# Sums of squares in a transformer kernel: six of eight tiles gathered on VectorE before TensorE sums them

## The reference

```python
def rms_norm_2(x, g):
    xf = xf * lax.rsqrt(jnp.mean(xf * xf, axis=-1, keepdims=True) + RMS_EPS)
    return (xf * g.astype(jnp.float32)).astype(x.dtype)

def pre(x_in, i):
    return rms_norm_2(x_in, norm_pre[l, i]) * (1.0 + mod[:, i, 1]) + mod[:, i, 0]

def post_add(x_in, y, i, res_w):
    return x_in + res_w * mod[:, i, 2] * rms_norm_2(y, norm_post[l, i])
```

## Time and profile before

| | |
|---|---|
| median of 3 runs | 3460.66 us (3459.83 to 3464.83) |
| profiled execution, first to last instruction | 3460.6 us (the profile gives no other time for it) |
| TensorE busy | 98% |
| VectorE, ScalarE, GpSimd busy | 47%, 35%, 13% |
| mean granted TensorE clock | 0.993 |

### The profile page before, as it was taken

The page is one execution under the profiler, slowest core; times in us unless marked ns, Lnnn a source line. Parts: engine busy times, 40 slices in busy tenths (PEclk is TensorE's granted clock), DMA queues, the critical chain, the costliest instruction groups (busy, mean ns, idle before and its releaser), DMA issues.

```text
span 3460.6 us, 38984 instructions
## 1 busy us (share of the span) xinstructions
PE 3388.4 (98%) x16286; PEld 2652.6 (77%) x16286; DVE 1630.0 (47%) x2132; ACT 1223.9 (35%) x1770; POOL 432.9 (13%) x338
## 2 busy tenths in 40 slices
PE   8999999999999999999999999999999999999998
PEld 6755477788888888887587888878888876878886
DVE  5555566443335635564334534475446533452233
ACT  3364465332223232224533322233323245332222
POOL 0100012121220100112011100110101210210001
PEclk9999999999999999999999999999999999999999
DMA  5412643234333334223032344333422322222221
GB/s 191 146 43 84 186 177 133 110 128 146 142 138 113 107 137 136 74 110 116 19 122 98 128 146 146 134 114 110 151 104 68 123 91 68 86 86 98 97 89 58
DMA packets 78353, 393.43 MB, mean 114 GB/s; under 512 B 8416, under 2 KB 17120, under 8 KB 45024
## 3 DMA queue, kind: packets, MB, share of 16 engines
q1 hardware_dynamic: 66048, 370.41, 30.9%
q10 hardware_dynamic: 12128, 20.52, 1.7%
HBM read 372.02 MB, written 18.87 MB: 113 GB/s over the span
## 4 chain that ended last, share of the span: by engine, by line
PE 93%; DVE 3%; ACT 2%; issue 1%; DMA 0%; POOL 0%; SPq 0%; DVEq 0%; ACTq 0%; POOLq 0%
PE pb L705 22%; PE pb L707 22%; PE pb L706 22%; PE pb L612 3%; PE pb L673 2%; PE pb L674 2%; PE pb L610 2%; PE pb L681 2%; PE pb L869 1%; PE pb L887 1%; PE pb L737 1%; PE pb L848 1%; DVE wl L2013 1%; PE pb L1200 1%; PE pb L1150 1%
## 5 line engine op out<-in xcount | busy, mean ns | idle before, releaser
L2013 DVE TENSOR_TENSOR wl<-w,wh 128x2048 fp32r<-128x2048 f32 (+3 forms) x264 | 582.2, 2205 | 898.3 <-ACT wh L1328 895.9
L705 PE MATMUL pb<-XH,wh 128*128 128x512 f32 (+1 forms) x2488 | 984.5, 396 | 2.3 <-DVE wl L2013 1.6
L707 PE MATMUL pb<-XH,wl 128*128 128x512 f32 (+1 forms) x2488 | 969.3, 390 | 0.0
L706 PE MATMUL pb<-XL,wh 128*128 128x512 f32 (+1 forms) x2488 | 969.0, 389 | 0.0
L1328 ACT ACTIVATE wh<-w 128x2048 fp32r<-128x2048 f32 (+3 forms) x264 | 471.5, 1786 | 294.3 <-PE pb L707 195.0
L705 PEld LDWEIGHTS pb<-XH,wh 128*128 128x128 f32 (+1 forms) x2488 | 465.6, 187 | 107.4 <-issue 8.2
L706 PEld LDWEIGHTS pb<-XL,wh 128*128 128x128 f32 (+1 forms) x2488 | 465.6, 187 | 101.2 <-issue 4.5
L707 PEld LDWEIGHTS pb<-XH,wl 128*128 128x128 f32 (+1 forms) x2488 | 465.2, 187 | 100.4
L2954 POOL TENSOR_TENSOR HL<-tmps,HH 128x512 fp32r<-128x512 f32 x120 | 165.8, 1384 | 1319.0 <-ACT HH L1650 1319.0
L705 PE MATMUL pb<-HH,wh 128*128 128x512 f32 x768 | 306.6, 399 | 0.0
L707 PE MATMUL pb<-HH,wl 128*128 128x512 f32 x768 | 303.7, 395 | 0.0
(11 more groups left out here) (472 smaller groups left out, 4061.4 us busy)
## 6 DMA issues: line engine op xcount, KB each, us to landing
w<-in_f_in SPq DMA_DIRECT2D x88, 1024.0 KB, 5.0
mreg<-in_mod_w SPq DMA_DIRECT2D x144, 512.0 KB, 3.6
w<-in_f_out SPq DMA_DIRECT2D x32, 1024.0 KB, 4.9
w<-in_w_up SPq DMA_DIRECT2D x16, 1024.0 KB, 5.7
w<-in_w_dn SPq DMA_DIRECT2D x16, 1024.0 KB, 5.7
w<-in_m_g SPq DMA_DIRECT2D x16, 1024.0 KB, 5.0
w<-in_f_out SPq DMA_DIRECT2D x16, 768.0 KB, 4.2
w<-in_w_rm SPq DMA_DIRECT2D x8, 1024.0 KB, 5.7
```

Of the source, the lines that this page charges most:

```text
L705: mm(dst, hi[:, cs], xh[:, k, :], start=k == 0, stop=False)
L706: mm(dst, hi[:, cs], xl[:, k, :], start=False, stop=False)
L707: x = mm(dst, lo[:, cs], xh[:, k, :], start=False, stop=fin)
L2013: tt(low[:, 0:s.cols], wslots[b % 3][:, 0:s.cols], h[:, 0:s.cols].bitcast(F32), ALU.subtract).then_inc(*DV.up(("lo", b), ("w_free", b)))
```

## The change

In each of the seven stages the squares of tiles 0 to 5 are first added on VectorE, elementwise, and TensorE sums only the result, once, after tile 6. Tiles 6 and 7 are summed as before. For "mlp" one buffer (`tmps[4]`) takes the plain sum: one add per tile, ahead of `add_h`. For the other six, `gather` keeps two buffers: `tmps[6]` the plain sum, and `tmps[7]` the sum weighted with `wsum[:, n, 1]`: for tile 1 three instructions, for tiles 2 to 5 two each. `gather` for tile j-1 is called at tile j, from `y_out`, `mo_out` or `add_last`. Those are `fn` of `evict`, so they come after the `lo` of that tile. TensorE waits for `("gathered", r, 5)` after tile 6, then `gathered_sums` runs eight one-column matmuls. ScalarE's squares wait for the gather that reads their buffer instead of for TensorE's sums.

```diff
+            def gathered_sums():
+                for a, factor in enumerate((c("mcol"), c("one"))):
+                    for i in range(4):
+                        mm(banks[3][:, 2 * i + a:2 * i + a + 1], tmps[6 + a][:, i * 128:(i + 1) * 128], factor,
+                           start=a == 0 and i == 0, stop=False, skip_group_check=True)
...
                     j = next(tile)
-                    for k in ([j - 1] if j else []) + ([7] if j == 7 else []):
+                    if j == 6:
+                        pe.wait_ge(*at("gathered", r, 5))
+                        token_sums(banks[3], tmps[4], 512, True, False)
+                    for k in (6, 7) if j == 7 else ():
                         pe.wait_ge(*at("sq", r, k))
-                        token_sums(banks[3], tmps[k % 4], 512, k == 0, k == 7).then_inc(*TE.up(("sq_mm", r, k)))
+                        token_sums(banks[3], tmps[k % 4], 512, False, k == 7).then_inc(*TE.up(("sq_mm", r, k)))
...
-                    if j == 0:
-                        pe.wait_ge(*at("wsum", name))
-                    else:
-                        pe.wait_ge(*at(label, name, j - 1))
-                        pair_sums(j - 1).then_inc(*TE.up(("pair", name, j - 1)))
+                    if j == 6:
+                        pe.wait_ge(*at("gathered", name, 5))
+                        gathered_sums()
+                    elif j == 7:
+                        pe.wait_ge(*at(label, name, 6))
+                        pair_sums(6)
...
-                    act.wait_ge(*at("pair", r, j - 2))
+                    act.wait_ge(*at("gathered", r, max(j - 2, 1)))
...
+            def add_o(j, o, bank):
+                if 2 <= j <= 6:
+                    n = j - 1
+                    dve.wait_ge(*at("sq", "mlp", n))
+                    if n > 1:
+                        dve.wait_ge(*at("gathered", "mlp", n - 1))
+                    tt(tmps[4][:, :], tmps[0 if n == 1 else 4][:, :], tmps[n % 4][:, :], ALU.add).then_inc(
+                        *DV.up(("gathered", "mlp", n)))
+                add_h(j, o, bank)
+
+            def gather(r, label, n):
+                if not 1 <= n <= 5:
+                    return
+                dve.wait_ge(*at(label, r, n))
+                if n > 1:
+                    dve.wait_ge(*at("gathered", r, n - 1))
+                    tt(tmps[6][:, :], tmps[6][:, :], tmps[n % 2][:, :], ALU.add).then_inc(*DV.up())
+                else:
+                    dve.wait_ge(*at("wsum", r))
+                    ts(tmps[7][:, :], tmps[0][:, :], wsum[:, 0, 1:2], None, ALU.mult).then_inc(*DV.up())
+                    tt(tmps[6][:, :], tmps[0][:, :], tmps[1][:, :], ALU.add).then_inc(*DV.up())
+                    own()
+                stt(out=tmps[7][:, :], in0=tmps[n % 2][:, :], scalar=wsum[:, n, 1:2], in1=tmps[7][:, :], op0=ALU.mult,
+                    op1=ALU.add).then_inc(*DV.up(("gathered", r, n)))
...
                     def y_out(j, o, bank):
+                        if q == 2 and r != (1, 2):
+                            gather(r, "y_sq", j - 1)
                         if q > 0:
                             dve.wait_ge(*at("mm", o))
...
                 def mo_out(j, o, bank):
+                    gather(r, "y_sq", j - 1)
                     dve.wait_ge(*at("ev", o))
                     dot(r, j)
```

More of the change, by code:

```diff
@@ L737, in pair_sums @@
                     x = mm(banks[3][:, 2 * i:2 * i + 2], tmps[j % 2][:, i * 128:(i + 1) * 128], wsum[:, j, :],
-                           start=j == 0 and i == 0, stop=False, skip_group_check=True)
+                           start=False, stop=False, skip_group_check=True)
                 return x
+            def gathered_sums():
[3 more added lines that the diff above has]
+                           start=a == 0 and i == 0, stop=False, skip_group_check=True)
             def spread(r, n, bank=4, factors=rcol):
@@ L1373, in fn @@
                     if j >= 4:
-                        act.wait_ge(*at("sq_mm", r, j - 4))
+                        act.wait_ge(*at("gathered", r, max(j - 4, 1)))
                     actf(tmps[j % 4][:, :], hT[:, j, :], ACT.Square).then_inc(*AC.up(("sq", r, j)))
@@ L1382, in final_square @@
                 if j >= 2:
-                    act.wait_ge(*at("pair", "final", j - 2))
+                    act.wait_ge(*at("gathered", "final", max(j - 2, 1)))
                 actf(tmps[j % 2][:, :], hT[:, j, :], ACT.Square).then_inc(*AC.up(("sq", "final", j)))
@@ L2374, in add_h, with add_last @@
                 tt(hT[:, j, :], hT[:, j, :], bank[:, :], ALU.add).then_inc(*DV.up(("ev", o)))
-            run(st_of["o"], add_h)
+            def add_o(j, o, bank):
[21 more added lines that the diff above has]
+                    op1=ALU.add).then_inc(*DV.up(("gathered", r, n)))
+            def add_last(j, o, bank):
+                gather("final", "sq", j - 1)
+                add_h(j, o, bank)
+            run(st_of["o"], add_o)
             norm("mlp", "g_mlp", HIGH_FIRST)
@@ L2382, in _ @@
                 run(st_of[("up", q)])
-                run(st_of[("dn", q)], add_h)
+                run(st_of[("dn", q)], add_last if q == 3 else add_h)
             while ticks < mod_end:
```

## The result

The changed kernel takes 3480.07 us (median of 5, 3477.95 to 3487.89) against 3460.66 before: ratio 1.0058, 95% interval 1.0046 to 1.0071. The forecast was 3472.5 with a range to 3480.0. So the direction was right, and the loss was larger than said, just past the end of the range: 19.4 us between the medians, 17.7 between the spans of the profiled executions, against 12.

A forecast was written before the change was run, and what follows sets the result against it. TensorE, busy 3388.4 of 3460.6 us, was taken as the bound. Removing 26 us of its calls against VectorE stalls summed to +5.6 us, clock loss added +6.4: +12 on 3460.7 gave 3472.5 us, range 3458 to 3480.

The forecast's parts named there:

- what is late next: At tile 6, gather 5 stands behind the next stage's low part on VectorE; tile 7 and the link wait for gather 5.
- The idle ahead of the sums: TensorE's stalls before `gathered_sums`, counted as 0.8 + 4.1 + 2 x 5.7 + 9.4 + 2 x 2.1 = 30 us.
- The bank wait in (0,2): In (0,2), tile 6 waits for a bank from 54.3 until VectorE's add ends at 56.1.
- GpSimd's share of one gather: A VectorE gather right behind a dot runs beside GpSimd's addition and loses up to 0.9 us, taken in full.
- The sum without GpSimd: All stages without GpSimd's share and without clock loss: some +1 us, 3461; stalls without clock loss had chance 0.22.
- the 0.9s of (0,0) and (1,0): GpSimd's share in these stages, each forecast at +2.1 us; without the 0.9s it would be +0.3.
- the 0.6s of the mixer stages: In (0,1) and (1,1), the low part takes 2.29 and some 0.6 us more beside GpSimd; -1.5 us each.
- the clock term: Four stages idling 4 us or more each lose 1.6 us to the slow clock: +6.4 us, bounds 0 and 11.
- the last rival: Removed calls' waits cost more than 0.885 us, so more is gained; 2.6 us of idle made it worth nothing; no chance given.
- without clock the sum: Stages without clock loss: -3.7 + 0.5 + 4.2 + 7.6 - 3.0 = +5.6 us; as a rival 3466, chance 0.22.
- The plain subtraction: Rival: VectorE takes the new 50 us in idle time, 26 us gained, 3435; chance 0.12, whole or half.
- that rival's second half: Half of the plain subtraction: gathers cheaper, GpSimd yields, stalls near 20, giving 3450 to 3453; within the shared chance 0.12.

The follow-up runs named there:

- Gathers first: Changed kernel with VectorE's gather of tile j-1 moved ahead of the slab's low part at tile j: 3447.6 us, ratio 0.9957 to the kernel before.
- small gathers: Changed kernel with gathers 2 to 5 of the six two-buffer stages on one column instead of 512: 3456.5 us, ratio 0.9979 to the kernel before.
- GpSimd off: Changed kernel with GpSimd's five additions of the dots per stage on one column instead of 512: 3468.31 us, ratio 1.0018 to the kernel before.
- the filler: Changed kernel with dense one-pass filler matmuls on TensorE ahead of its wait for gather 5 in the six two-buffer stages: 3461.19 us, ratio 0.9998.
- the best version: Changed kernel with gathers ahead of the low parts, (0,2) summed tile by tile as before the change: 3438.02 us, ratio 0.9925 to the kernel before.
- the last version with sums late: Changed kernel with gathers ahead of the low parts and the two buffers' sums behind tile 7: 3449.48 us, ratio 0.9957 to the kernel before.
- the short version: Gathers ahead of low parts, (0,2) tile by tile, plus 7 filler matmuls ahead of the wait in (0,0) and (1,0): 3437.95 us, ratio 0.9927.

## Why the prediction was right and wrong

**Right: what is late next.** That gather 5 stands behind the next stage's low part, and tile 7 behind gather 5, was the decisive step. Gathers first and small gathers show it from both sides. The idle ahead of the sums was forecast at 0.8, 4.1, 5.7, 9.4, 5.7 and twice 2.1, together 30. Measured: 0.6, 3.35, 5.1, 8.65, 5.1 and twice 1.3, together 25.5. The bank wait in (0,2) was there (1.5, forecast 1.8).

**Right: GpSimd's share of one gather.** "So a gather right behind a dot loses up to 0.9; I take it in full": the scaled add took 1.79 instead of 0.75, and 0.74 with GpSimd off. The sum without GpSimd, "+1", was too high: it takes off the 0.9s of (0,0) and (1,0) and the 0.6s of the mixer stages, 4.8, but nothing in (0,2). With GpSimd off the profiled execution was 9.6 us shorter, 4.0 of it in (0,2); part of it is the clock, whose mean went from 0.986 to 0.988.

**Wrong: the clock term.** "I take one such stretch for each, +6.4." The runs give 19 us, the difference that the filler makes; by the table 0.9 in "final", then 3.8, 3.6, 4.2, 3.5 and 3.2. Two things were mis-sized. The price of a dip: 1.6 us is the price of one 3.4 us long. Behind the four long idles they were 10.2 to 13.7 us long, of which only the part that fell into the idle cost nothing. In (0,0) the small matmuls took 3.4 us for 1.7, and the clock did not rise while they ran, so tile 7 paid too, 6.4 for 4.2: 3.9 in all. And the number of stages: all six paid, also the mixer stages at 1.3 us of idle (dips of 6.8 us), which I had at nothing. Why the dips are so much longer than the one of the earlier trace rows stays open. In the mixer stages the idle is shorter than there (1.3 against 1.57 us) and the dip longer, so it is not the length of the idle alone. The small matmuls behind each idle may be the reason; no run has a long idle without them.

**Wrong: a removed wait priced at zero.** "The rows show 2.6 us of idle before all of them, so this is worth nothing", said the last rival. But 1.8 of the 2.6 stood ahead of two calls that the change removes, and the row counts the idle of the matmuls alone; their weight loads waited longer. The timeline of the kernel before, (0,1), behind tile 1:

```profile
1847.33 1.28 ACT L1365 ACT_TABLE_LOAD   x1
...
1848.73 0.61 ACT L1701 ACTIVATE tmps<-YT 128x512 f32<-128x512 f32 x1
...
1849.40 0.97 PEld L737 LDWEIGHTS pb<-cols,tmps 128*128 128x128 f32 x8 [1.33 <-ACT tmps L1701]
```

The first call sat behind a table load of ScalarE, 1.3 us, and went away with the change. From the matmul ahead of it to the one behind it are 2.21 us, in the stage's later calls 1.03: 1.2 us more in each mixer stage. In (0,0), (0,2) and (1,0) the first call took 0.3 more than the later ones. Together that is 3.3 us not counted, and the idles ahead of the sums came to 4.5 less than forecast. The two are about the size of the gap: without clock the sum was +5.6, and with the filler the span is 1.7 under before. How much of the 4.5 reached the end was not tested alone. So one error of +13 and one of -7 stood against each other. That the forecast missed by only 6 to 8 us is partly luck.

**The plain subtraction**, 26 us, was about the right size for what TensorE's calls are worth: the best version has 22.7 of it between the spans, with one stage (3.6) left out. In that rival's second half a sum does not come out: 26 us less with stalls near 20 give some 3455, not 3450 to 3453.

## What to carry to other kernels

Before giving an idle engine extra work, look not at its busy share but at what stands ahead of that work in its queue at the moment the busy engine asks. Here the same adds cost 0.6% behind a slab's low part and gain 0.4% ahead of it. A stall of a dense TensorE stream can cost more than its length. Here each of six cost 1 to 4 us more, as small matmuls behind it and most of the next tile ran at half clock, and filler took that back. In other places the length of the dip has to be measured. Price each stage by itself; the one that cannot take the work (ticks, one slab more, short tiles) is better left out.

## What was not expected of the hardware

- Behind the idles of 3.35 to 8.65 us in the changed kernel the granted clock stayed at its lower level for 10.2 to 13.7 us from where it fell, including all of the small matmuls behind the idle. With GpSimd off, the same idle of 3.05 was followed by 6.8 us of it in (0,0) and by 10.2 in (1,0).
- It also fell with no idle ahead of the sums, in the last version with sums late, after small matmuls alone had kept TensorE busy for 2.5 us in (0,0) and 3.2 in (1,0); it then stayed at 0.50 for 10.2 us in both links. Eight such matmuls alone, with no idle ahead, had no dip behind them in the mixer stages of the kernel with gathers first. Filler of 512 columns in one pass kept the clock up in most places, but not in "final" and, in the short version, not in (0,0), where 3.4 us of dip followed.
- The same idle of 1.3 us was followed by sums of 1.8 us in one kernel and of 2.6 to 2.9 in another, and with GpSimd off by 1.8 in one mixer stage and 2.9 in the other. Why, could not be told from the rows.
- In the changed kernel a GpSimd addition and a scaled add of VectorE that ran beside each other both lengthened: 1.68 instead of 1.27 to 1.30 on GpSimd, 1.78 instead of 0.75 on VectorE.
